# Strassen's seven products in the output projection of a hybrid attention and recurrence block

## What is computed

```
h    = rmsnorm(x, w_norm_pre)
proj = h @ w_in                  # 1024 -> q_a, k_a, v_a, z_a, q_r, f_r, i_r, z_r (3328 columns)
o_a  = sliding_window_sink_attention(rope(q_a), rope(k_a), v_a) * silu(z_a)      # 8 heads of 64
o_r  = rmsnorm(hgrn2_chunkwise(q_r, f_r, i_r), hgrn_norm) * silu(z_r)            # 4 heads of 128
y    = concatenate([o_a, o_r]) @ w_out     # 2048 x 1024 times 1024 x 1024
x    = x + rmsnorm(y, w_norm_post)
```

## Time and profile before

| | us |
|---|---|
| median of 3 runs | 876.72 |
| lowest, highest | 874.83, 877.73 |
| span of the profiled execution (first to last instruction) | 872.4 |
| TensorE busy | 862.6 (99%) |
| VectorE busy | 592.9 (68%) |
| ScalarE busy | 499.3 (57%) |
| GpSimd busy | 115.7 (13%) |
| share of TensorE in the chain of work that ended last | 88% |
| moved by DMA: 186.03 MB, mean 213 GB/s | |

### The profile page before, as it was taken

One profiled execution on the slowest core, in us unless ns is written; L12 is line 12 of the kernel. 1 busy time (PEld: TensorE's weight loads), 2 busy tenths in 40 slices (PEclk: granted clock), 3 DMA queues, 4 the chain that ended last, 5 costly groups with the idle time before them and its releaser, 6 DMA issues.

```text
span 872.4 us, 12348 instructions
## 1 busy us (share of the span) xinstructions
PE 862.6 (99%) x4478; PEld 709.9 (81%) x4478; DVE 592.9 (68%) x1061; ACT 499.3 (57%) x1009; POOL 115.7 (13%) x90
## 2 busy tenths in 40 slices
PE   8999999999999999999999999999999999999997
PEld 6887788888888788888888878888888877788886
DVE  6878867764756798867163679878625468977823
ACT  7766456663574559657147546866624655667532
POOL 0000013430200001342020000243111000013112
PEclk9999999999999999999999999999999999999999
DMA  8685755639968544552785644446379545444463
GB/s 319 236 307 205 265 199 180 250 145 365 418 229 286 221 170 145 177 185 99 289 328 201 241 172 166 146 146 211 130 262 338 193 147 176 154 151 146 161 245 126
DMA packets 52924, 186.03 MB, mean 213 GB/s; under 512 B 5888, under 2 KB 6144, under 8 KB 52864
## 3 DMA queue, kind: packets, MB, share of 16 engines
q1 hardware_dynamic: 50128, 178.29, 57.2%
q10 hardware_dynamic: 2736, 6.95, 2.0%
HBM read 141.18 MB, written 44.04 MB: 212 GB/s over the span
## 4 chain that ended last, share of the span: by engine, by line
PE 88%; DVE 5%; DMA 3%; ACT 2%; issue 1%; SPq 1%; POOL 0%; DVEq 0%; ACTq 0%
PE bank L478 61%; PE bank L487 8%; PE score_b L487 4%; PE turn_b L487 4%; DMA kept_lo<-w_lo 2%; PE score_b L507 2%; PE turn_b L531 2%; PE turn_b L584 2%; PE bank L565 2%; PE turn_b L587 1%; PE bank L575 1%; DVE q_gate L1305 1%; PE turn_b L521 1%; DMA x_in<-in_x 1%; DVE w_lo L997 1%
## 5 line engine op out<-in xcount | busy, mean ns | idle before, releaser
L478 PE MATMUL bank<-h_hi,w_lo 128*128 128x512 f32 x832 | 327.1, 393 | 0.0
L478 PE MATMUL bank<-h_lo,w_hi 128*128 128x512 f32 x832 | 325.9, 392 | 0.0
L478 PE MATMUL bank<-h_hi,w_hi 128*128 128x512 f32 x832 | 324.5, 391 | 0.8 <-ACT h_hi L790 0.8
L478 PEld LDWEIGHTS bank<-h_lo,w_hi 128*128 128x128 f32 x832 | 156.3, 188 | 34.5 <-issue 3.3
L478 PEld LDWEIGHTS bank<-h_hi,w_hi 128*128 128x128 f32 x832 | 156.3, 188 | 33.6 <-ACT h_hi L790 1.3
L478 PEld LDWEIGHTS bank<-h_hi,w_lo 128*128 128x128 f32 x832 | 156.2, 188 | 33.1 <-issue 0.2
L1341 POOL TENSOR_TENSOR mix_lo<-v_r,mix_hi 128x512 fp32r<-128x512 f32 x16 | 21.2, 1323 | 522.6 <-ACT v_r L911 522.6
L997 DVE TENSOR_TENSOR w_lo<-w_raw,w_hi 128x1024 fp32r<-128x1024 f32 x37 | 45.8, 1248 | 32.8 <-ACT w_hi L736 32.6
L1119 DVE STREAM_TRANSPOSE kv_tok<-k_mid 32x128 f32<-32x128 f32 x192 | 58.0, 302 | 2.8
L736 ACT ACTIVATE w_hi<-w_raw 128x1024 fp32r<-128x1024 f32 x38 | 39.7, 1050 | 22.1 <-issue 9.9
L487 PE MATMUL bank<-w_hi,mix_lo 128*128 128x512 f32 x128 | 50.5, 395 | 0.0
(11 more groups left out here) (189 smaller groups left out, 1467.4 us busy)
## 6 DMA issues: line engine op xcount, KB each, us to landing
w_hi<-kept_hi SPq DMA_DIRECT2D x96, 512.0 KB, 3.7
w_lo<-kept_lo SPq DMA_DIRECT2D x96, 512.0 KB, 4.7
w_raw<-in_weights SPq DMA_DIRECT2D x38, 512.0 KB, 5.4
kept_hi<-w_hi SPq DMA_DIRECT2D x34, 512.0 KB, 6.5
kept_lo<-w_lo SPq DMA_DIRECT2D x34, 512.0 KB, 7.1
x_in<-in_x_rows SPq DMA_DIRECT2D x8, 1024.0 KB, 7.2
x_in<-in_x SPq DMA_DIRECT2D x15, 512.0 KB, 5.9
out<-q_gate ACTq DMA_DIRECT2D x9, 512.0 KB, 8.5
```

Source lines behind the costliest of these rows:

```text
L478: mm = pe.matmul(acc(w)[:, :], stationary[:, s, k, :], moving[:, k, :], start=(m == 0), stop=(m == 3 * KT - 1), skip_group_check=True)
```

## The change

From sequence tile 1 on (`FAST` = 1) the output projection is made by Strassen's scheme. The 512 x 1024 values are cut into 2 x 2 blocks of 256 tokens by 512 values, the weights into 2 x 2 blocks of 512 by 512, and seven products of 256 x 512 x 512 (`P1` to `P7`, each 24 matmuls) take the place of eight: 168 matmuls in place of 192. Sequence tile 0 stays as it was (`out_plain`).

*Units.* `UNITS` is the order of 56 units of three matmuls, (weight tile, k, token block i). There are now 14 weight tiles for the output projection (`P1A` to `P3B`, w = 26 to 39, `FAST_WT` = 40), each used for 12 matmuls. Six banks are used: two (`x_bank`) take P1, P6, P5 and P3 one onto the other, each read out by ScalarE (`keep`) in between; two (`w_bank`) take P7 and, onto it, P4; two (`y_pair`) take P2. VectorE adds a bank to a kept copy (`took`), scales (`post`) and adds the residual (`finish_y`).

*Sums of values.* Of the attention half, VectorE makes one difference of 1024 columns (`s3`); of the recurrence half, `sum_head` makes three sums of 256 columns per head, ScalarE their high parts (`s_high`), GpSimd the low ones (VectorE for the last head).

*Sums of weights.* Four combinations of the blocks of w_out (8 weight tiles, `T1` to `T4`) are made once, in sequence tile 1, in two halves: SyncE loads four raw tiles (`load_sums`, at w = 6 and w = 13), GpSimd subtracts four times and later makes four low parts (`sum_weights`, at its steps 5 and 11), ScalarE makes the high parts (`sums_high`, two at each of steps 7, 8, 13 and 14), and SyncE saves eight times 512 KB in DRAM (`save_sums`, at w = 11 and w = 18). The second load waits for the first saves.

*Slots and order of loads.* From tile 1 on every weight tile has slot w % 4. The residual is now loaded at w = 38 (P3A) and w = 39 (P3B), each after that weight tile's own load. The order of finishing and storing is blocks 2, 3, 0, 1.

```diff
+FAST_ROWS = [B11, B11 + 1, T3, T3 + 1, B21, T2, T4, B21 + 1, T2 + 1, T4 + 1, T1, T1 + 1, B22, B22 + 1]
+FAST_WT = OUT0 + len(FAST_ROWS)
+SPLIT_SLOT = SPLIT_SLOT + [w % 4 for w in range(FAST_WT)] * (TILES - FAST)
+UNITS = [(w, k, i) for w, ks in ((P1A, (0, 1)), (P1B, (2, 3)), (P7A, (0, 1)), (P7B, (2, 3)), (P2A, (0, 1)), (P6A, (0, 1)), (P4A, (0, 1)))
+         for k in ks for i in range(2)]
+UNITS += [(w, k, i) for k in (2, 3) for w in (P2B, P6B, P4B) for i in range(2)]
+UNITS += [(P5A, k, i) for k in (0, 1) for i in range(2)] + [(P5B, k, i) for i in range(2) for k in (2, 3)]
+UNITS += [(w, k, i) for i in range(2) for w, ks in ((P3A, (0, 1)), (P3B, (2, 3))) for k in ks]
+SUMS_IN, SUMS_OUT = (6, 13), (11, 18)
+SUMS_AT = (5, 11)
...
+            def load_sums(j):
+                if j == 0:
+                    sp.wait_ge(lo_split.sem, lo_split.after(0, 0) + FRESH - 1)
+                else:
+                    sp.wait_ge(t_saved, 16 * T_TILES)
+                for r, w in enumerate((B11, B21, B12, B22)):
+                    sp.dma_start(w_raw[:, r, :, :], weights[(w + j) * P:(w + j + 1) * P, :].rearrange("p (k m) -> p k m", k=KT)).then_inc(t_raw, 16)
+            def save_sums(j):
+                sp.wait_ge(t_high, 4 * (j + 1))
+                sp.wait_ge(t_low, 4 * (j + 1))
...
+                    if t == FAST and w in SUMS_IN:
+                        load_sums(SUMS_IN.index(w))
+                    if t == FAST and w in SUMS_OUT:
+                        save_sums(SUMS_OUT.index(w))
-                    if w == WT - 3:
+                    if w == (P3A if t >= FAST else WT - 3):
                         load_residual(t, 0)
-                    if w == WT - 1:
+                    if w == tiles_of(t) - 1:
                         load_residual(t, 1)
...
+            def out_fast(t):
+                for n, (w, k, i) in enumerate(UNITS):
+                    for part, mix, weight, into in unit(t, w, k, i):
+                        m = 3 * n + part
+                        between(t, OUT0 + m // 21, m % 21)
+                        if part == 0:
+                            unit_waits(t, n, w, k, i)
+                        mm = pe.matmul(into, mix, weight, start=w in (P1A, P7A, P2A) and k == 0 and part == 0,
+                                       stop=k == KT // 2 - 1 and part == 2, skip_group_check=True)
...
+            def keep(t, i, src, dst):
+                act.activation(dst, src, ACT.Copy).then_inc(y_kept.sem, 1)
+            def sums_high(k):
+                act.wait_ge(t_sum, k + 1)
...
+                    if t == FAST:
+                        for j, first in enumerate(SUMS_AT):
+                            for k in (0, 1) if s == first + 2 else (2, 3) if s == first + 3 else ():
+                                sums_high(4 * j + k)
...
+            def sum_weights(j):
+                raw = lambda r: w_raw[:, r, :, :]
+                pool.wait_ge(t_raw, 64 * (j + 1))
+                for k, (dst, a, b) in enumerate(((0, 2, 0), (2, 3, 2), (3, 3, 0), (1, 1, 3))):
...
+                    pool.tensor_tensor(raw(dst), raw(a), raw(b), ALU.subtract).then_inc(t_sum, 1)
```

More of the change, by code:

```diff
@@ L307, in wait_slot @@
                 return
-            tile, v = divmod(before(i), WT)
-            if v in (OUT0 + 3, WT - 1):
+            tile, v = where(before(i))
+            if tile >= FAST:
+                engine.wait_ge(tile_done.sem, tile_done.after(tile, v))
+            elif v in (OUT0 + 3, WT - 1):
                 engine.wait_ge(y_done.sem, y_done.after(tile, 3 if v == OUT0 + 3 else 7))
@@ new lines, in unit @@
+            def unit(t, w, k, i):
+                even, odd = slice(i * P, (i + 1) * P), slice((2 + i) * P, (3 + i) * P)
+                if w in (P1A, P1B, P7A, P7B):
+                    cols = even if w in (P1A, P1B) else odd
+                    hi, lo = mix_hi[:, k, cols], mix_lo[:, k, cols]
+                elif w in (P2A, P2B, P4A, P4B):
+                    cols = even if w in (P2A, P2B) else odd
+                    hi, lo = mix_hi[:, QT + k, cols], mix_lo[:, QT + k, cols]
+                else:
+                    which = S2 if w in (P6A, P6B) else S1 if w in (P5A, P5B) else S4
+                    hi, lo = s_hi[:, which, k, even], s_lo[:, which, k, even]
+                into = w_bank if w in (P7A, P7B, P4A, P4B) else y_pair if w in (P2A, P2B) else x_bank
+                slot, half = SPLIT_SLOT[index(t, w)], slice(4 * (k % 2), 4 * (k % 2) + 4)
+                for part in range(3):
+                    mix, weight = ((hi, w_hi), (lo, w_hi), (hi, w_lo))[part]
+                    yield part, mix, weight[:, slot, half, :].rearrange("p a m -> p (a m)"), into[i][:, :] if len(into[i].shape) == 2 else into[i]
@@ new lines, in out_fast @@
+            def out_fast(t):
[7 more added lines that the diff above has]
+                                       stop=k == KT // 2 - 1 and part == 2, skip_group_check=True)
+                    if w not in [v for v, _, _ in UNITS[n + 1:]]:
+                        mm.then_inc(tile_done.sem, 1)
+                    elif w in (P6B, P5B, P3B) and k == KT // 2 - 1 and i == 0:
+                        mm.then_inc(half_done.sem, 1)
@@ L901, in _ @@
                             place_probs(t, 3, 8)
+                    if t >= FAST and s == out_step(HEADS - 1):
+                        act.wait_ge(tile_done.sem, tile_done.after(t, P1B))
+                        for i in range(2):
+                            keep(t, i, x_bank[i], p1[i])
                     for head in range(HEADS):
@@ L914, in _ @@
                             rstd(t, score_b[:, 1, :], o_scale[:, :], P).then_inc(o_rstd.sem, 1)
+                            if t >= FAST and head == HEADS - 1:
+                                act.wait_ge(tile_done.sem, tile_done.after(t, P7B))
+                                for i in range(2):
+                                    keep(t, 2 + i, w_bank[i][:, :], p7[i])
                     for head in range(HEADS):
@@ L936, in _ @@
                         act.activation(v_win[:, 1::2, :], turned_v, ACT.Copy).then_inc(v_win_ready.sem, 1)
-                    for j in MIXA.get(s, ()):
+                    if t >= FAST and s in MIXA:
+                        first = MIXA[s][0] == 0
+                        act.wait_ge(gated.sem, gated.after(t, PAIRS - 1)) if first else act.wait_ge(a_sum.sem, a_sum.after(t, 0))
+                        if t == FAST and first:
+                            act.wait_ge(t_saved, 16 * 2 * T_TILES)
+                        act.activation(mix_hi[:, 0:QT, 0:2 * P] if first else mix_hi[:, 0:QT, 2 * P:], a11 if first else s3,
+                                       ACT.Copy).then_inc(mixa_hi.sem, 2)
+                    for j in MIXA.get(s, ()) if t < FAST else ():
                         act.wait_ge(gated.sem, gated.after(t, PAIRS - 1))
@@ L1246, in _ @@
                                           ALU.mult).then_inc(gated.sem, 1)
+                        if q == PAIRS and t >= FAST:
+                            dve.wait_ge(gated.sem, gated.after(t, PAIRS - 1))
+                            dve.tensor_tensor(s3, a11, a21, ALU.subtract).then_inc(a_sum.sem, 1)
                     for h in range(HEADS):
```

381 lines of the change are left out of this document (295 added, 86 removed).

## The result

The changed kernel takes **906.0 us** (median of 4 runs, 902.3 to 906.7) against 876.3 in the same session: a ratio of 1.0327, 95% interval 1.0302 to 1.0351. The forecast was slower, 889.1 (868 to 897). The direction was right; of the +29.7 us it had +12.4.

The account below looks back on a forecast made before the run. TensorE was taken as the bound, busy 862.6 of 872.4 us. The span 872.4 + 9.9 + 0.5 + 0.5 + 1.5 gave 884.8; the same 12.4 on the median 876.7 gave 889.1 us, range 868 to 897.

Parts of the forecast that it names:

- Products, -16.3: Output projections of the three fast tiles: 24 matmuls fewer each, 5.44 us a tile, 16.3 us less TensorE work.
- Weights of the output projection: Fast output projections: late weight and residual transfers eat the saving; +0.5 us in tiles 1 and 2, +1.5 at the end.
- P3A's landing: Output projection: P3A lands 2.8 us behind P5B, at 429.2, in time for its use at 429.6.
- The wait of 1.9 us for the next tile's first weights: End of tile 1's output projection: next weights land at 441.0, TensorE is through at 439.1.
- Sums, first half: Tile 1: raw loads delay a save and the loads of weight tiles 7, 8 and 9; +4.6 us, at least 2.
- Sums, the rest: Tile 1: ScalarE waits for late sums ahead of block copies, delaying the exponentials; 9.9 us late, first half's 4.6 included.
- The upper bound of 13: Tile 1, all sums of weights: at most 13 us, if memory is slower when written and read at once.
- At nothing: head sums: Fast tiles: head sums and copies fit VectorE's and ScalarE's gaps and cost nothing; uncovered, 1 to 2 us a tile.
- A: Rival, tile 1: the sums of weights are hidden, only 2.1 us stay; 881.3 us, chance 0.15.
- B: Rival: the output projection runs at TensorE's pace, each fast tile keeps its 5.4 us; 870.3 us, chance 0.15.
- D: Rival: four waits of about 4 us also cost clock, another 2 us each; 897 us, chance 0.08.

Follow-up runs that it names:

- c1: a1 plus the four raw loads of the first half in tile 1, which nobody uses; 892.8 us.
- d2: The changed kernel with GpSimd's sixteen subtractions and ScalarE's eight copies for the sums of weights cut to 16 columns per block; 893.6 us.
- b3: The changed kernel with ScalarE's high parts of the weight sums moved behind the block copies and exponentials; 908.5 us.
- c2: a1 plus sixteen GpSimd subtractions of 128 x 1024 on old data in tile 1, whose results nobody waits for; 894.2 us.
- a1: The changed kernel with the sums of weights left out (no raw loads, subtractions, high parts or saves); 888.0 us.
- c4: The changed kernel without sums of weights, residual loads moved in all fast tiles, VectorE's sums of values on 16 of 256 columns in tiles 2 and 3; 872.1 us.
- a4: The changed kernel with twelve unused matmuls put ahead of P3B's first unit in each fast tile; 905.1 us.
- b1: The changed kernel with 10, 8 and 16 unused matmuls put into three of TensorE's waits in tile 1; 905.0 us.
- d1: The changed kernel without sums of weights, residual loads moved in all fast tiles, low parts of output weights loaded only to a quarter from tile 1 on; 869.4 us.

## Why the prediction was right in direction and wrong in size

*Products, -16.3.* Right (4478 to 4406 matmuls). That none of it reaches the time was right too, and for the reason given.

*Weights of the output projection, forecast +0.5, +0.5, +1.5; measured +2.3, +2.0, +3.3.* The mechanism was right: P3B lands behind the first residual, TensorE waits 3.4 to 3.5 us for it in each fast tile, and the second residual holds the end of the last tile. The step mis-sized is P3A's landing. Single transfers of tile 1 (issue us, then us to landing), beside the earlier trace rows: P3A, first residual, P3B, second residual.
```profile
L450 SPq DMA_DIRECT2D w_lo<-kept_lo x1: 432/432/432, 446.4 to 446.4; - x1
DMA to landing us min/median/max: 7.9/7.9/7.9
...
L486 SPq DMA_DIRECT2D x_in<-in_x_rows x1: 448/448/448, 446.9 to 446.9; - x1
DMA to landing us min/median/max: 10.0/10.0/10.0
...
L450 SPq DMA_DIRECT2D w_lo<-kept_lo x1: 445/445/445, 448.0 to 448.0; - x1
DMA to landing us min/median/max: 11.3/11.3/11.3
...
L486 SPq DMA_DIRECT2D x_in<-in_x_rows x1: 884/884/884, 448.5 to 448.5; - x1
DMA to landing us min/median/max: 13.4/13.4/13.4
```
They land at 454.3, 456.9, 459.3 and 461.9: 7.6 us for three, better than the 2.8 and 3.1 each that were taken. But P3A lands 4.6 us behind P5B (449.7), forecast 2.8: P5B and P3A were issued only 1.4 us apart, when the queue was not yet full (DMA share 0.64 from 444 to 450). From 449.7 to 454.3 the share was 0.97 and 1.7 MB moved, more than P3A has, so part of it went to the transfers behind. I had summed as if six megabytes stood in the queue from P5B on, one landing behind another. Counted from the start of the projection P5B lands at 34.2 us (forecast 33.1), P3A at 38.8 (35.9) and P3B at 43.8 (41.8); P3B's 2.0 us, less 0.2 behind it, are what lies between +0.5 and +2.3. The wait of 1.9 us for the next tile's first weights did not come; TensorE, waiting 1.5 us more for P3A and then at the lower clock (0.82 in 459.4 to 467.4), reached them no earlier than they landed.

*Sums, first half, forecast +4.6.* Right in kind and chain: `c1` gives 4.8 us (6.1 in the stage), weight tile 8 is waited for, and the loads behind the saves go out at 261.9, 270.9 and 279.8, 9.0 apart (forecast 9.7 and 8.8). That the number fits so well is in part luck. Forecast were 2.4 us before weight tile 8 and 2.2 more before tile 9; measured were 0.6 and 3.4 before tiles 7 and 8, none before tile 9, and 1.7 lost to the clock, for which the sum had no term.

*Sums, the rest, forecast +5.3, with the first half 9.9; measured 18.4 in all.* Here the prediction failed. It found the right chain, and blamed the wrong engine for it: ScalarE's eight copies cost 2.3 us of the stage (`d2`; the forecast had 2.1 for two of them), but its waiting for late sums is not borne out by `b3`. The step that failed is the pricing of GpSimd's subtractions only by when their results come; they also stop VectorE, which is in that chain. `c2` prices that alone at 6.2 us of time, with the clock behind the wait that it makes. The upper bound of 13 had no term for it. The trace of before could have told. VectorE's line 1268 in tile 2 of the kernel before:
```profile
542.06 0.43 DVE L1268 TENSOR_SCALAR f_a<-f_b 128x512 f32<-128x512 f32 x1
...
566.74 1.55 DVE L1268 TENSOR_SCALAR f_a<-f_b 128x512 f32<-128x512 f32 x1
```
and GpSimd's at the second of these times, while it is idle at the first:
```profile
566.72 1.28 POOL L1351 TENSOR_TENSOR mix_lo<-h_mix,mix_hi 128x512 fp32r<-128x512 f32 x1 [2.23 <-ACT mix_hi L892]
```
The same instruction takes 0.43 or 1.55 us, by whether GpSimd began 0.02 us ahead of it. All 16 of the line are one or the other, eight each. I had read GpSimd's 2.5 us per subtraction and never what VectorE did beside it.

*At nothing: head sums.* Wrong, at the upper end that the text itself named: +2.1 and +1.9 us in tiles 1 and 2 (`a1`), 0.1 in tile 3. About half of it in tile 2 is the width of the operations (`c4`), so the cover named (gaps between a head's steps) is not whole there. Why tile 3, with the same operations, loses nothing is not shown; it has no next tile whose squares GpSimd would add beside them.

*Rivals.* A and B did not come. D came in kind and, wait by wait, nearly in size; the forecast's sum had no term for it: behind each long wait of tile 1 the clock fell to 0.76 to 0.79 over 8 us, 1.7 to 1.9 us of work each where the rival said 2. The Trainium skill's rule that idleness halves the clock (TensorE: Matmul & The Clock Gate, "Part 1: The HAM clock gate") is borne out by these rows. But little of it came back in `a4` and `b1`: 0.9 and 1.0 us of time, no more than the runs of one kernel differ. Of the missed 17.3 us (29.7 less 12.4), tile 1's input projection has 10.6, the output projections and the end 5.1, tile 2's input projection 1.9; the sum, 17.6, is 0.3 off, less than the entry varies.

Open: whether GpSimd's operations cost more where their results are waited for (8.2 us of the stage, give or take what it varies) than where they stand alone (6.7); how much of the 5.3 us of clock in tile 1 could be had back; and the last 1.3 us of the output projections in `d1` against the 41.5 of 24 matmuls fewer.

## To carry to other kernels

A scheme that saves products and needs more distinct operands moves work from TensorE to the transfers: divide the bytes of a weight tile by the matmuls it serves before counting matmuls. Work given to an idle engine is not free if it shares a way into memory with one on the path; look at the spread of a line's durations, not at its mean, and price the slower neighbour. A wait of some us of TensorE costs clock behind it as well: give it a term in the sum. In a chain of waits, move or shrink the suspect before believing the order that the timeline shows: ScalarE's wait looked like the cause, and without it the kernel was no faster.

## What the runs showed of the hardware

- VectorE's operations with two operands in SBUF, and its scalar one of line 1268, take up to one GpSimd operation (1.9 to 2.4 us for 1024 columns) longer beside it: 3 columns 1.94 us and not 0.12, 1024 columns 3.22 and not 1.23; even 16 columns 1.15. The operation on 3 columns ended 0.02 us behind GpSimd's. It goes the other way too: GpSimd's of 323.80, which began while VectorE's of 3.22 was running, took 3.23 and not 2.40. Reductions, transpositions and operations that read a bank kept their times (1.22, 5.04, 0.68).
- With four and more megabytes queued, they land about 2.5 us apart (413 GB/s); a lone one takes 4.8 to 5.1 from its issue (issued at 393.3 and 400.2 before the change, at 444.7 after it: 5.0, 5.1 and 5.0; at 413.3: 4.8).
- After waits of 2.5 to 5.2 us the granted clock of the next 8 us was 0.66 to 0.82; filling the waits with unused matmuls restored it in the output projection (1.00) and at two of three places of tile 1, and returned about 1 us in either kernel.
